# Modulation sums of a transformer kernel redistributed over TensorE, VectorE and GpSimd

## What is computed

```python
c_act = silu(c)
mod = c_act @ mod_w[layer] + mod_b[layer]
sh1, sc1, g1, sh2, sc2, g2 = split(mod, 6)
u = rms_norm(h, norm_mix) * (1 + sc1) + sh1
h = h + g1 * mixer(u)
u = rms_norm(h, norm_ffn) * (1 + sc2) + sh2
h = h + g2 * ((silu(u @ wg) * (u @ wu)) @ wo)
shift, scale = split(c_act @ kv_mod_w + kv_mod_b, 2)
```

## Time and profile before

| | |
|---|---|
| runs | 2532.32, 2536.72, 2539.07 us (median 2536.72) |
| span of the profiled execution | 2522.8 us |
| TensorE (PE) busy | 2247.2 us, 89% |
| VectorE (DVE) busy | 1459.4 us, 58% |
| ScalarE (ACT) busy | 768.2 us, 30% |
| GpSimd (POOL) busy | 569.8 us, 23% |
| mean granted TensorE clock | 0.947 |

### The profile page before, as it was taken

How to read it: one execution, slowest core, us unless ns; L and a number is a source line. 1 busy time by engine, 2 the same in 40 slices (tenths; PEclk the granted TensorE clock), 3 DMA queues, 4 the chain that set the end, 5 groups by cost and what they waited for, 6 DMA issues and landing times.

```text
span 2522.8 us, 25247 instructions
## 1 busy us (share of the span) xinstructions
PE 2247.2 (89%) x9944; PEld 1787.3 (71%) x9944; DVE 1459.4 (58%) x1747; ACT 768.2 (30%) x983; POOL 569.8 (23%) x340
## 2 busy tenths in 40 slices
PE   3689889889999998999989999969888876999996
PEld 0567767768888887766778888748466665788885
DVE  7766665666767674345444444573544665655556
ACT  2342223323222223345332222244223232322221
POOL 5342231366988860000000000000410000000000
PEclk9899989989999998999999999979888988999998
DMA  5332121234454542211122222202012221222220
GB/s 204 133 134 101 53 98 67 100 134 163 171 198 175 182 166 90 94 61 38 52 83 100 93 92 100 101 36 103 14 50 84 101 70 64 84 101 99 87 98 34
DMA packets 39644, 252.64 MB, mean 100 GB/s; under 512 B 4563, under 2 KB 4755, under 8 KB 11048
## 3 DMA queue, kind: packets, MB, share of 16 engines
q1 hardware_dynamic: 33176, 234.11, 25.4%
q0 software_dynamic: 3008, 10.63, 1.3%
q10 hardware_dynamic: 3344, 6.29, 0.7%
HBM read 244.73 MB, written 6.29 MB: 99 GB/s over the span
## 4 chain that ended last, share of the span: by engine, by line
PE 81%; DVE 13%; issue 3%; ACT 2%; DMA 0%; POOL 0%; DVEq 0%; SPq 0%; ACTq 0%; POOLq 0%
PE bank L620 23%; PE bank L621 22%; PE bank L622 22%; PE bank L807 2%; PE bank L909 2%; PE bank L919 1%; DVE scr L1546 1%; PE bank L897 1%; DVE w_lo L1516 1%; DVE pool L1712 1%; PE bank L732 1%; PE bank L726 1%; DVE scr L1584 1%; PE bank L988 1%; DVE scr L1709 1%
## 5 line engine op out<-in xcount | busy, mean ns | idle before, releaser
L620 PE MATMUL bank<-u_hi,w_hi 128*128 128x512 f32 x1772 | 713.9, 403 | 44.0 <-DVE u_lo L1578 12.3
L621 PE MATMUL bank<-u_lo,w_hi 128*128 128x512 f32 x1772 | 699.7, 395 | 0.0
L622 PE MATMUL bank<-u_hi,w_lo 128*128 128x512 f32 x1772 | 698.5, 394 | 0.0
L1516 DVE TENSOR_TENSOR w_lo<-raw,w_hi 128x2048 fp32r<-128x2048 f32 x165 | 433.2, 2625 | 282.6 <-ACT w_hi L1082 282.5
L620 PEld LDWEIGHTS bank<-u_hi,w_hi 128*128 128x128 f32 x1772 | 339.3, 191 | 126.0 <-issue 48.4
L1082 ACT ACTIVATE w_hi<-raw 128x2048 fp32r<-128x2048 f32 x165 | 314.9, 1908 | 329.0 <-PE bank L622 326.0
L622 PEld LDWEIGHTS bank<-u_hi,w_lo 128*128 128x128 f32 x1772 | 338.6, 191 | 72.8
L621 PEld LDWEIGHTS bank<-u_lo,w_hi 128*128 128x128 f32 x1772 | 339.6, 192 | 66.8 <-issue 0.2
L620 PE MATMUL bank<-g_hi,w_hi 128*128 128x512 f32 x708 | 281.7, 398 | 33.4 <-DVE scr L1652 18.9
L535 POOL TENSOR_TENSOR raw<-raw,cact 128x2048 f32<-128x2048 f32 x53 | 193.3, 3647 | 387.2 <-DMA raw<-in_wts 368.8
L621 PE MATMUL bank<-g_lo,w_hi 128*128 128x512 f32 x708 | 278.8, 394 | 0.0
(11 more groups left out here) (248 smaller groups left out, 2345.9 us busy)
## 6 DMA issues: line engine op xcount, KB each, us to landing
raw<-in_wts SPq DMA_DIRECT2D x221, 1024.0 KB, 4.8
spectra<-pool ACTq DMA_DIRECT2D x16, 256.0 KB, 2.0
pool<-in_rel POOLq DMA_DIRECT2D x16, 256.0 KB, 2.9
pool<-spectra POOLq DMA_DIRECT2D x16, 256.0 KB, 3.0
H<-in_x ACTq DMA_DIRECT2D x1, 2048.0 KB, 21.2
out<-H SPq DMA_DIRECT2D x1, 2048.0 KB, 7.1
pool<-in_window POOLq DMA_DIRECT2D x1, 1024.0 KB, 8.8
pool<-in_filt_w POOLq DMA_DIRECT2D x1, 512.0 KB, 6.2
```

The costliest lines, as they stand in the source:

```text
L620: pe.matmul(out, lh, rh, start=start, stop=False, skip_group_check=True)
L621: pe.matmul(out, lh, rl, start=False, stop=False, skip_group_check=True)
L622: return pe.matmul(out, ll, rh, start=False, stop=stop, skip_group_check=True)
L1516: dve.tensor_tensor(w_lo[w % hi_ring][:, :], raw[W_STREAM[w] % raw_ring][:, :], w_hi[w % hi_ring][:, :].bitcast(F32), ALU.subtract).then_i ...
```

## The change

The eight first modulation slots are contracted wholly on TensorE, 16 matmuls of one column each, in the filter network and beside the taps of the first filter (`direct_mod`). The next twelve are summed by VectorE, one step of the sum at each of the eight hooks of the first twelve slots of the mixer. GpSimd sums only the last 36, and begins when the input of the first FFN has been split. In the stream the first eight slots now stand together ahead of the spectrum slots, the next twelve one behind each mixer slot from the second on, none in the output projection, one behind each slot of the first FFN (two behind `fi0` 1), and four behind the key slots. The points at which VectorE takes vectors move with them. The two ScalarE passes of each filter layer become one VectorE operation.

```diff
+M_DIRECT = 8
+M_HOOKED = 12
+M_POOLED = M_DIRECT + M_HOOKED
...
-    s.extend([("M",)] * 5)
-    one("spec", 0, 1)
-    one("spec", 1, 2)
-    one("spec", 2)
-    one("spec", 3)
-    for label, i in A_SLOTS:
-        one(label, i, 2 if label == "v0" else 1 if label == "g0" else 0)
-    w("wo0", 4, 1)
+    s.extend([("M",)] * M_DIRECT)
+    for i in range(4):
+        one("spec", i)
+    for idx, (label, i) in enumerate(A_SLOTS):
+        one(label, i, 1 if 1 <= idx <= M_HOOKED else 0)
+    w("wo0", 4)
...
-            m = 1 if layer == "0" and left[0] else 0
+            m = min(left[0], 2 if label == "fi" and i == 1 else 1) if layer == "0" else 0
...
-    for x in ("kk", "vv", "qq", "wo1"):
+    w("kk", 4, 1)
+    for x in ("vv", "qq", "wo1"):
...
+MOD_POINTS = [(M_DIRECT, 2), (M_POOLED, 5), (24, 6), (52, 13), (NM, NVMOD)]
...
-                pl.wait_ge(m_done, M_START)
-                for m in range(M_START, NM):
+                pl.wait_ge(u_l, U_FFN0 + KC)
+                for m in range(M_POOLED, NM):
...
+            def direct_mod(m):
+
+                s = M_STREAM[m]
+                src = raw[s % raw_ring]
+                pe.wait_ge(cact_ready, 1)
+                pe.wait_ge(raw_in[s % raw_ring], 16 * (s // raw_ring + 1))
+                for j in range(2):
+                    for k in range(KC):
+                        c = k * 256 + j * P
+                        mm = pe.matmul(bank[7][:, 2 * m + j:2 * m + j + 1], src[:, c:c + P], cact[:, k:k + 1],
+                                       start=(k == 0), stop=(k == KC - 1))
+                mm.then_inc(mod_sum, 1)
...
                 complete(mm, i)
+                direct_mod(i)
...
+                    if o == 0:
+                        direct_mod(3 + t)
+                if o == 0:
+                    direct_mod(7)
...
-                act.activation(f_a[0:FH, 0, :], b[0:FH, :], ACT.Identity, bias=vcol("filt_b", i)[0:FH]).then_inc(free["act"], 1)
-                act.wait_ge(free["act"], i + 1)
-                act.activation(f_a[0:FH, 1, :], f_a[0:FH, 0, :], ACT.Identity, bias=zcol[0:FH, 0:1],
-                               scale=vcol("filt_fr", i)[0:FH]).then_inc(f_arg, 1)
...
+            def sum_mod(m, k):
...
+                if k == 0:
+                    dve.wait_ge(cact_ready, 1)
+                    dve.wait_ge(raw_in[s % raw_ring], 16 * (s // raw_ring + 1))
...
+                    dve.tensor_scalar(acc, src[:, 0:256], cact[:, 0:1], None, ALU.mult).then_inc(m_step, 1)
+                else:
+                    dve.wait_ge(m_step, (KC - 1) * (m - M_DIRECT) + k)
                     ins = dve.scalar_tensor_tensor(acc, src[:, k * 256:(k + 1) * 256], cact[:, k:k + 1], acc, ALU.mult, ALU.add)
...
-                dve.wait_ge(f_arg, i + 1)
+                dve.tensor_scalar(a, read(i)[0:FH, :], vcol("filt_b", i)[0:FH], vcol("filt_fr", i)[0:FH],
+                                  ALU.add, ALU.mult).then_inc(free["dve"], 1)
+                dve.wait_ge(*free_of(i))
...
-                sum_mod(i)
...
                     if k == 2:
                         ahead(label, i)
+                    if idx < M_HOOKED:
+                        sum_mod(M_DIRECT + idx, k)
...
-            take_mods(MODS_WO0)
+            take_mods(MODS_FFN0)
...
-            take_mods(MODS_ALL)
+            take_mods(MODS_KV)
             modulated("kv", NORM["kv"], U_KV, KSC, KSH)
...
+            take_mods(MODS_ALL)
```

More of the change, by code:

```diff
@@ L152 @@
 NM = len(M_BEFORE)
-M_START = 3
 NVMOD = NM // 4
@@ L157 @@
 SCALES = {SC1_0: (0, "norm_mix0"), SC2_0: (1, "norm_ffn0"), KSC: (2, "kv_norm"), SC1_1: (3, "norm_mix1"), SC2_1: (4, "norm_ffn1")}
-MODS_MIX0, MODS_WO0, MODS_FFN0, MODS_OUT0, MODS_ALL = range(5)
-MOD_POINTS = [(sum(b <= w for b in M_BEFORE), v) for w, v in (
-    (W_AT[("spec", 3)], 2), (W_AT[("g0", 3)], 4), (W_AT[("wo0", 3)], 5), (W_AT[("fo0", 0)] - 1, 6), (NW, NVMOD))]
+MODS_MIX0, MODS_FFN0, MODS_OUT0, MODS_KV, MODS_ALL = range(5)
+MOD_POINTS = [(M_DIRECT, 2), (M_POOLED, 5), (24, 6), (52, 13), (NM, NVMOD)]
+assert sum(b <= W_AT[("fo0", 0)] - 1 for b in M_BEFORE) == 24
+assert sum(b <= W_AT[("kk", 0)] for b in M_BEFORE) == 52
 def plan_outputs():
@@ L188, in part @@
         used[W_AT[slot]] = events[0]
-    out("filt", 3, "act")
+    out("filt", 3, "dve")
     for o in (0, 1):
@@ L501, in _ @@
                     kind, n = where[s - raw_ring]
-                    sp.wait_ge(lo_done if kind == "W" else m_done, n + 1)
+                    if kind == "W":
+                        sp.wait_ge(lo_done, n + 1)
+                    elif n < M_DIRECT:
+                        sp.wait_ge(mod_sum, n + 1)
+                    else:
+                        sp.wait_ge(*summed(n))
                 if item[0] == "W":
@@ L539, in sum_mods @@
                         pl.wait_ge(mod_sum, m - MRING + 1)
-                    pl.tensor_tensor(macc[:, m % MRING, :], src[:, 0:256], src[:, 256:512], ALU.add).then_inc(m_done, 1)
+                    pl.tensor_tensor(macc[:, m % MRING, :], src[:, 0:256], src[:, 256:512], ALU.add).then_inc(m_pooled, 1)
             pl.memset(zcol[:, 0:1], 0.0).then_inc(const_ready, 1)
@@ L641, in mods @@
             def mods(w):
-                for m in range(NM):
+                for m in range(M_DIRECT, NM):
                     if M_BEFORE[m] == w:
-                        pe.wait_ge(m_done, m + 1)
+                        pe.wait_ge(*summed(m))
                         for sums, vectors in MOD_POINTS:
@@ L1600, in residual @@
                 dve.scalar_tensor_tensor(H[:, c, :], b[:, :], mcol(gate, c), H[:, c, :], ALU.mult, ALU.add).then_inc(free["dve"], 1)
-            def sum_mod(m):
+            def sum_mod(m, k):
                 s = M_STREAM[m]
                 src, acc = raw[s % raw_ring], macc[:, m % MRING, :]
-                dve.wait_ge(cact_ready, 1)
-                dve.wait_ge(raw_in[s % raw_ring], 16 * (s // raw_ring + 1))
-                if m >= MRING:
-                    dve.wait_ge(mod_sum, m - MRING + 1)
-                link(dve.tensor_scalar(acc, src[:, 0:256], cact[:, 0:1], None, ALU.mult))
-                for k in range(1, KC):
+                if k == 0:
+                    dve.wait_ge(cact_ready, 1)
+                    dve.wait_ge(raw_in[s % raw_ring], 16 * (s // raw_ring + 1))
+                    if m >= MRING:
+                        dve.wait_ge(mod_sum, m - MRING + 1)
+                    dve.tensor_scalar(acc, src[:, 0:256], cact[:, 0:1], None, ALU.mult).then_inc(m_step, 1)
+                else:
+                    dve.wait_ge(m_step, (KC - 1) * (m - M_DIRECT) + k)
                     ins = dve.scalar_tensor_tensor(acc, src[:, k * 256:(k + 1) * 256], cact[:, k:k + 1], acc, ALU.mult, ALU.add)
-                    if k < KC - 1:
-                        link(ins)
-                    else:
-                        ins.then_inc(m_done, 1)
+                    ins.then_inc(m_hooked if k == KC - 1 else m_step, 1)
             dve.wait_ge(vec_in, 16)
```

9 lines of the change are left out of this document (5 added, 4 removed).

## The result

The changed kernel takes 2492.4 us (median of four runs, 2490.8 to 2499.8), the kernel before 2536.4 beside it (2532.3 to 2539.1): a ratio of 0.984, 95% interval 0.983 to 0.986. The two medians lie 44 us apart; the ratio puts the gain at 1.4 to 1.7%, 36 to 44 us. The forecast was 2504, faster by 33 us.

A forecast was written before the change was run, and what follows sets the result against it. TensorE was taken as the bound (VectorE at the start), losing time to VectorE stalls beside GpSimd and the low clock. Terms 2 - 50 - 5 + 14 + 6 = -33 us gave 2504 us; own range 2487 to 2521, eight in ten 2472 to 2532.

The forecast's parts named there:

- The mixer: HGRN2 mixer, 166.6 to 504 us: minus 50 us, as up to 63 us go and new VectorE steps cost 13.
- 268 + 6 + 13 = 287 us: Mixer: 268 us TensorE work at 2.4 GHz, about 6 of waits not from GpSimd, 13 (bounds 3 and 38) for hooked steps.
- The output projection and its norm: 504 to 568 us: minus 5 us because four GpSimd sums leave; bounds 2 and 8.
- The start: Direct slots at 1.2 GHz, 7.1 us each; sine slot done 6.5 us later; net plus 2, bounds minus 34 and plus 8.
- The 4.2 us that I took off for the norm after it: First modulated norm after the start: its u_lo no longer stands for GpSimd, 4.2 us put on the path.
- The first FFN: Plus 14 us: GpSimd begins late, so TensorE waits about 13.5 us for the fourth weight slot; bounds 8 and 18.
- The key norm: 942 to 960 us: plus 6 us from two collisions of L1546 and L1555 with GpSimd's sums; bounds 0 and 9.
- 13.9 us "around the span": Profiled span 2522.8 lies 13.9 us under the runs' median 2536.7, taken as launch and carried over to the forecast time.
- Start at 2.4 GHz: Rival, start: direct slots cost 3.2 us, sine slot ends at about 79; 36 us less, 2468 us; chance 0.16.
- Steps show in the hooks: Rival, mixer: hooked steps delay the next level, 38 instead of 13 us of new waits; 2529 us; chance 0.14.
- Direct sums serialize: Rival, start: matmuls into one PSUM column wait for each other, 12 to 19 us per slot; 2543 to 2599; chance 0.07.
- Nothing in the mixer: Rival, mixer: stalls come from something other than GpSimd, so the change does nothing there; about 2555 us; chance 0.03.

The follow-up runs named there:

- lumped: Changed kernel with all eight VectorE steps of a mixer sum at the last hook of its slot instead of one at each hook: 2505.0 us, ratio 0.991.
- The experiment with one early sum: Changed kernel with only the first of GpSimd's last 36 sums free to start when its slot has landed: 2487.5 us, ratio 0.983.
- the repetition: Both kernels run once more, unchanged: the kernel before 2535.6 us (ratio 1.001), the changed kernel 2495.9 us (ratio 0.986).
- The second pair: Profiled executions of the kernel before and the changed kernel, each run once more unchanged; measured times 2535.6 and 2495.9 us.
- the short start: Changed kernel with each direct slot cut to its last chunk, 2 of 16 matmuls, so most of the sums are left out: 2455.6 us, ratio 0.971.
- the shared start: Changed kernel with direct slots 1, 3, 5 and 7 summed by VectorE in eight steps each, TensorE only reducing them: 2480.9 us, ratio 0.979.

## Why the prediction was right, point by point

**The mixer: right, and most of the cause shown.** Forecast -50 from its second slot to the output projection. The second slot starts at 169.7 instead of 166.7, the projection's first matmul at 456.7 instead of 508.4: -54.7. Giving the twelve sums back to GpSimd costs 40.1 of them; the other 15 have no experiment of their own (before, the sums also stood at other places of the stream). The 5 us missed are a boundary: my row ended at 504, 4.4 us before the projection, while the sum 268 + 6 + 13 = 287 us holds all the mixer's work. The stretch measured 287.0:

```profile
169.70:456.70 287.00, 274.44 (x1555) 232.59 (x1553) 195.60 (x419) 102.93 (x126) 0.00 (x0) 1.00 0.30 103
```

That it is met so closely is luck. My 13 us for the steps were too much, since TensorE's waits for L1739 are 3.3 us in all. The work was too cheap (busy 274.4 us instead of 268), and so were the other waits (9.2 instead of 6). That the spacing matters was right: lumped, they cost 16.6.

**The output projection and its norm: right.** Forecast -5; from the projection's first matmul to the norm's first step it is 53.0 us instead of 57.3, -4.3. With the mixer that is -59.0 where I had -55.

**The start: right in both directions.** Forecast +6.5 at the end of the sine slot; the taps behind it and the norm's broadcast start at 116.35 instead of 109.94, +6.4. The cosine slot starts at 87.23, forecast 88.3; a direct slot took 7.0 us, forecast 7.1. The 4.2 us that I took off for the norm after it: the second slot of the mixer is 3.0 later, so 3.4 came back. The u_lo operations that took up to 4.01 us all take 0.75 now. The level was right, my reason for it was not: I had said that loads keep the array busier than products, but from 31 to 88 us the loads are busy 46.6 us and the products 57.0. Why the level stays low there is open.

**The first FFN: the size right, the telling not.** Forecast +14: split of the first key slot at 900.07 instead of 942.11, which is +14.0 behind a norm 56.0 earlier. But I had put one wait of 13.5 us before the fourth weight slot, for GpSimd's third sum. The trace has its longest wait, 6.8 us, before the third (ScalarE's casts, then the split that TensorE waits for, then TensorE at the start of its second, third and fourth slot and inside its fifth):

```profile
538.00 1.91 ACT L1114 ACTIVATE w_hi<-raw 128x2048 fp32r<-128x2048 f32 x1 [10.59 <-DMA raw<-in_wts]
...
554.07 1.92 ACT L1114 ACTIVATE w_hi<-raw 128x2048 fp32r<-128x2048 f32 x1 [5.55 <-DMA raw<-in_wts]
...
539.95 4.54 DVE L1543 TENSOR_TENSOR w_lo<-raw,w_hi 128x2048 fp32r<-128x2048 f32 x1 [13.20 <-ACT w_hi L1114]
...
526.20 0.50 PE L634 MATMUL bank<-u_hi,w_hi 128*128 128x512 f32 x1 [0.93 <-DVE w_lo L1543]
...
544.54 0.79 PE L634 MATMUL bank<-u_hi,w_hi 128*128 128x512 f32 x1 [6.81 <-DVE w_lo L1543]
...
558.98 0.48 PE L634 MATMUL bank<-u_hi,w_hi 128*128 128x512 f32 x1
...
580.68 0.71 PE L634 MATMUL bank<-g_hi,w_hi 128*128 128x512 f32 x1 [1.93 <-DVE H L1627]
```

Its load stands on SP's queue behind the load of modulation slot 22, and that one waits until the *first* sum (done at 530.5) frees its buffer. I followed the buffer of the fourth slot and not the queue in front of the third. The fourth was ready at 558.8, 38.4 us after GpSimd's start (forecast 41.5). By then the second slot had lost 0.9 us and the third 6.8, and more at the granted clock of 0.50 from 540 to 550, so the fourth started at 558.98 without a wait. Counted from the FFN's first matmul it starts 9.5 us later than before (46.4 us instead of 36.9, which is 605.50 in the trace of before). Another 3.8 us come in the fifth slot: TensorE waits 1.9 us there for L1627 and runs slow behind it, a term that the forecast lacked. That the sum is 14 is in part luck. The experiment with one early sum rests on this reading: it freed the third slot (its cast at 534.08, no wait before it) and brought 10 of the 14 us.

**The key norm: right.** Forecast +6, measured +5.5, as two stretched squares (VectorE, beside GpSimd's L549 from 907.25 to 911.19):

```profile
908.31 3.43 DVE L1573 TENSOR_TENSOR scr<-scr 128x512 f32<-128x512 f32 x1
911.66 0.74 DVE L1627 SCALAR_TENSOR_TENSOR H<-bank,modc,H 128x512 f32<-128x512 f32 x1
912.32 3.84 DVE L1573 TENSOR_TENSOR scr<-scr 128x512 f32<-128x512 f32 x2
```

I had left out the sums after it. Those beside the key slots stretch splits there to 5.68 us, though TensorE waits for none of them. That stretch is 2.0 us longer in this pair and 1.7 in the repetition of both; by which path isn't shown.

**The step that failed: 13.9 us "around the span".** The terms gave -33 for the span, and it was -31.7. The time itself was 11.6 us below the forecast because I took the distance from the profiled span to the median for launch. It is about 2 us; the other 12 were a quick execution (12 below the first four runs' median, 6 below that of the 39 later ones). Against the median of before the change is worth more than my terms: 44 and, in the repetition, 36 us. So it is partly luck that the terms meet the difference of two spans: a quick execution of before stands beside an ordinary one of after. The second pair, 2533.8 and 2490.3, differs by 43.5, with 66.9 instead of 63.7 in the mixer and 6.4 in a last stretch that the change doesn't touch. The runs of either kernel scatter over 7 to 15 us.

**The rivals.** *Start at 2.4 GHz:* out; direct passes 0.22 apart, and not even dense passes between them changed it. *Steps show in the hooks:* out as they stand, right as a mechanism when lumped. *Direct sums serialize:* out; sixteen products of one slot, eight into one column, took 7.0 us, 0.218 a pass, as those of L726 did with 0.222. *Nothing in the mixer:* out.

## What to carry over

Look on each engine for what it blocks and not only for its own load: GpSimd was a spare engine by its busy share, but its operations could stop a VectorE operation with both operands in SBUF, and some of these stand on TensorE's path; 44 us of added VectorE work were cheaper than 105 us of "free" GpSimd work. When work is moved behind an in-order load queue with few buffers, follow the *queue*: the first load that is late is the one behind the first buffer that stays full, which need not be the buffer that you are thinking of. And before a span is compared with a median, take the launch from a run that has both; one profiled execution can lie 6 to 12 us beside the middle.

## What the runs showed of the hardware that I had not expected

TensorE stayed at its lower level through 57 us without a gap, with passes of one column and taps of 64 rows, and also with dense bf16 passes in between. The purely dense passes of the cosine slot, from 87.23 on, were at the upper level at 93. The column of the granted clock showed 1.00 throughout.

The last stretch, from about 1630 to the end, has the same matmuls in all kernels and took 856.8 to 867.5 us, the longer the lower its granted clock. The two ends of it, the short start and the shared start:

```profile
1594.00:2451.20 857.20, 747.67 (x3151) 590.38 (x3150) 475.14 (x615) 259.30 (x295) 43.88 (x80) 0.93 0.22 75
...
1612.00:2479.90 867.90, 758.51 (x3151) 596.35 (x3150) 475.16 (x615) 259.12 (x295) 43.81 (x80) 0.91 0.22 74
```

TensorE is busy 10.8 us longer with the same work, and no other engine is. So a gain of 10 us shows clearly only stretch by stretch. What decides how the clock falls in one execution wasn't tried.

A VectorE operation with a PSUM operand was not seen to stand beside GpSimd's (all 88 of L1627 between 509 and 925 us take 0.731 to 0.752 us, though GpSimd is busy 340 us of the FFN's 412; one of them starts at 907.65, inside an L549 that runs from 907.25 to 911.19), while those with both operands in SBUF were (the squares of 3.43 and 3.84 us at its side).
